# Opening on unscaled rows: the norm's factor applied behind the transposes and behind the first two projections

## The reference

```python
def rmsnorm(x, g):
    y = x * rsqrt(mean(x * x, axis=-1) + EPS)
    return y * g

h = rmsnorm(x, norm1_g)
z = h @ w_in                      # 1024 x 2824
u_s5, x_rg, g_rg, q, k, v, o, gi, gf = split(z)
mix = concat(s5(u_s5), rglru(x_rg, g_rg), mlstm(q, k, v, gi, gf, o))
x = x + mix @ w_out
x = x + moe(rmsnorm(x, norm2_g))  # top 4 of 32 experts
y = rmsnorm(x, final_norm_g)
# S5's coefficients, from small weights only:
step = exp(log_step)
mag = exp(lam_re * step)
ab = mag * cos(lam_im * step), mag * sin(lam_im * step)
```

## Time and profile before

| | us |
|---|---|
| runs, median of 3 | 1101.66 (1099.63 to 1101.93) |
| profiled execution | 1100.9 |
| its span | 1099.1 |

### The profile page before, as it was taken

How to read it: one execution, slowest core, us unless ns; L and a number is a source line. 1 busy time by engine, 2 the same in 40 slices (tenths; PEclk the granted TensorE clock), 3 DMA queues, 4 the chain that set the end, 5 groups by cost and what they waited for, 6 DMA issues and landing times.

```text
span 1099.1 us, 13174 instructions
## 1 busy us (share of the span) xinstructions
PE 1033.2 (94%) x5132; PEld 434.6 (40%) x5132; DVE 317.2 (29%) x643; ACT 198.4 (18%) x418; POOL 95.4 (9%) x177
## 2 busy tenths in 40 slices
PE   8999999999999998999899988999899989998986
PEld 5767745334333433343333323332334233433322
DVE  6889456312131212120212112121212121202123
ACT  6543525301110201011000201020102010100002
POOL 6899000000000000000000000000000000000000
PEclk9999999999999999999999999999999999999999
DMA  7533799999999999999999999999999999999995
GB/s 234 185 111 78 271 370 401 426 428 431 431 431 430 429 432 432 432 431 431 432 431 432 431 431 432 432 431 431 432 432 432 431 431 432 432 431 431 425 427 202
DMA packets 62052, 429.45 MB, mean 391 GB/s; under 512 B 12022, under 2 KB 25054, under 8 KB 33342
## 3 DMA queue, kind: packets, MB, share of 16 engines
q1 hardware_dynamic: 60868, 428.16, 93.3%
q10 hardware_dynamic: 1146, 0.79, 0.2%
HBM read 424.68 MB, written 3.67 MB: 390 GB/s over the span
## 4 chain that ended last, share of the span: by engine, by line
PE 53%; DMA 38%; DVE 5%; ACT 2%; issue 1%; SPq 1%; ACTq 0%; DVEq 0%
DMA ring_a<-in_exp_w_dram 32%; PE psum L2369 17%; PE psum L2404 12%; PE psum L2390 6%; DMA ring_b<-in_exp_w_dram 6%; PE psum L2303 3%; PE psum L2326 3%; PE psum L2134 3%; PE psum L1862 2%; PE psum L2413 1%; PE psum L2253 1%; PE psum L2259 1%; DVE rgb L1336 1%; SPq L444 1%; PE psum L2419 0%
## 5 line engine op out<-in xcount | busy, mean ns | idle before, releaser
L2369 PE MATMUL psum<-ring_a,xg 128*64 128x512 f32 x1200 | 341.8, 600 | 14.8 <-DMA ring_a<-in_exp_w_dram 14.8
L2404 PE MATMUL psum<-ring_a,aT 128*64 128x512 f32 x768 | 217.7, 596 | 9.9 <-DMA ring_a<-in_exp_w_dram 9.6
L2369 PEld LDWEIGHTS psum<-ring_a,xg 128*64 128x64 f32 x1200 | 102.8, 137 | 170.8 <-issue 165.4
L2369 PE MATMUL psum<-ring_b,xg 128*64 128x512 f32 x368 | 152.3, 598 | 7.7 <-DMA ring_a<-in_exp_w_dram 7.7
L1667 DVE TENSOR_TENSOR x<-x,psum 128x512 f32<-128x512 f32 x64 | 44.0, 687 | 384.1 <-PE psum L2326 384.1
L2390 PE MATMUL psum<-ring_a,xg 128*64 128x512 f32 x336 | 103.5, 609 | 14.5 <-DMA ring_b<-in_exp_w_dram 14.5
L2404 PEld LDWEIGHTS psum<-ring_a,aT 128*64 128x64 f32 x768 | 68.2, 137 | 111.8 <-issue 106.5
L2404 PE MATMUL psum<-ring_b,aT 128*64 128x512 f32 x256 | 104.1, 595 | 4.0 <-DMA ring_a<-in_exp_w_dram 2.5
L1736 DVE TENSOR_SCALAR acts<-psum 128x512 f32<-128x512 f32 x32 | 22.0, 687 | 224.4 <-PE psum L2390 208.0
L1040 ACT ACTIVATE acts<-acts 128x512 f32<-128x512 f32 x32 | 20.1, 627 | 297.5 <-DVE acts L1736 297.5
L2369 PEld LDWEIGHTS psum<-ring_b,xg 128*64 128x64 f32 x368 | 43.1, 136 | 75.5 <-issue 63.6
(11 more groups left out here) (504 smaller groups left out, 922.8 us busy)
## 6 DMA issues: line engine op xcount, KB each, us to landing
ring_a<-in_exp_w_dram SPq DMA_DIRECT2D x144, 2048.0 KB, 26.3
ring_b<-in_exp_w_dram SPq DMA_DIRECT2D x46, 2048.0 KB, 24.9
ring_a<-in_w_in_dram SPq DMA_DIRECT2D x4, 2048.0 KB, 8.5
ring_a<-in_w_out_dram SPq DMA_DIRECT2D x2, 2048.0 KB, 9.1
ring_a<-in_w_in_dram SPq DMA_DIRECT2D x3, 1024.0 KB, 5.8
ring_a<-in_state_ml_c_dram SPq DMA_DIRECT2D x4, 512.0 KB, 6.1
out_dram<-ring_a SPq DMA_DIRECT2D x4, 512.0 KB, 6.2
ring_b<-in_exp_w_dram SPq DMA_DIRECT2D x2, 1024.0 KB, 28.9
```

What stands on the lines that cost most here:

```text
L2369: m = M(psum[64 * x:64 * x + 64, bk, :], xg[:, k, u, 64 * x:64 * x + 64], w[x][:, 512 * bk:512 * bk + 512], start=False, stop=(k == KD - 1))
L2404: m = M(psum[64 * x:64 * x + 64, 4 + nn, :], aT[:, 2 * j + s, 64 * x:64 * x + 64], w[x][:, 1024 * s + 512 * nn:1024 * s + 512 * nn + 512], ...
```

## The change

TensorE turns the rows as they land, unscaled. All six halves are moved by VectorE, times the norm's weight, into `raw_hT`, which lies in the room of the later `qkT`. The root is taken once for all three tiles and inverted once. TensorE multiplies the factors, spread over 128 columns, by the identity: the bank rstd then holds in each partition the factor of each of the 288 rows. ScalarE copies it to `rstd_row`. VectorE multiplies `raw_hT` by it in two halves into `hT` (`scaled`). u0 and u1 are projected from `raw_hT` and scaled by VectorE as it moves them (`u_scaled`); ScalarE makes the rolled copy from `uT`. All later projections read `hT`.

The vectors are turned in two tiles: 24 rows and the S5 step first (`vec`), the others inside u0 (`vec2`). The step's exponential is taken on the two partitions of `step2` before it is spread. The matmuls of `keep_warm` go from 14, 1, 1 and 2 to 9 and 1. The left half of the first weights is issued ahead of five of the vector loads, the two lambdas ahead of both, the states' loads go from SyncE's queue to ScalarE's, the S5 output weights (`glw`) behind one block of input weights, and par is turned after xr0. The row's multiplications stand on VectorE between the angles and the coefficients for the first half, u0 and the second half; u1 stands behind the coefficients.

```diff
@@ -68,7 +69,9 @@
 _fills_of[b] += 1
-_place(["vec"] + [f"hT{i}" for i in range(6)] + ["u0", "u1", "par", "gp", "xr0", "gates", "xr1", "bt", "gr0", "ct", "gr1"], range(6))
+_place(["vec", "vec2"], (6,))
+_place(["rstd"], (7,))
+_place([f"hT{i}" for i in range(6)] + ["u0", "u1", "par", "gp", "xr0", "gates", "xr1", "bt", "gr0", "ct", "gr1"], range(6))
@@ -181,6 +183,7 @@
 hT = ms("hT", [128, KD, T])
+raw_hT = qkT[:].rearrange("p (k t) -> p k t", k=KD)
@@ -211,6 +214,7 @@
 uT_rolled = ms("uT_rolled", [128, 2, T])
+rstd_row = uT_rolled[:, 1, :]
@@ -458,6 +462,9 @@
     sp.dma_start(xn[0:TS, 2, :], a["x_sample"].rearrange("b t n -> (b t) n")).then_inc(sem("x_loaded2"), 16)
+    for name, src in LAMBDAS:
+        load_vector(sp, name, src)
+    sp.dma_start(slot_view(0, 512)[:, :, 0:256], w_in_cols(WCH[0][0], 256)).then_inc(sem("w_in0"), 16)
@@ -471,15 +478,10 @@
                     sp.dma_start(c_in[:, 2 * x + tt, :], a[name][0, 8 * tt:8 * tt + 8].rearrange("g c p -> (g c) p")).then_inc(sem("c_loaded"), 16)
-            for x, name in enumerate(("state_s5_re", "state_s5_im")):
-                sp.dma_start(srow[64 * x:64 * x + 64, :], a[name][0].rearrange("b (j g) p -> (b j) (g p)", g=2)).then_inc(sem("par_loaded"), 16)
-            sp.dma_start(prow[0:32, :], a["state_ml_n"][0].rearrange("b h k -> (b h) k")).then_inc(sem("par_loaded"), 16)
...
             sp.dma_start(m0[:], a["state_ml_m"][0].rearrange("b h -> h b")).then_inc(sem("gb_loaded"), 16)
+        if c == 2:
             sp.dma_start(glw[:], a["s5_glu_w"][0].rearrange("(k p) n -> p k n", p=128)).then_inc(sem("glw_loaded"), 16)
-        if c == 2:
@@ -494,9 +496,7 @@
         if c == 0:
-            for x in range(2):
-                sp.dma_start(slot_view(0, 512)[:, :, 256 * x:256 * x + 256], w_in_cols(WCH[0][0] + 256 * x, 256)).then_inc(
-                    sem(("w_in0", "w_in0_right")[x]), 16)
+            sp.dma_start(slot_view(0, 512)[:, :, 256:512], w_in_cols(WCH[0][0] + 256, 256)).then_inc(sem("w_in0_right"), 16)
@@ -655,6 +655,7 @@
     pool.wait_ge(*fill_ended("hT5"))
+    pool.wait_ge(*at("root_ready", 1))
@@ -722,32 +723,33 @@
     act.wait_ge(*at("nst_set", 1))
-    A(nst[:, 12:13], nst[:, 8:9], ACT.Sqrt).then_inc(says_now("table_loaded"), 1)
+    act.wait_ge(sem("step_loaded"), 16)
+    A(step2[:], step2[:], ACT.Exp).then_inc(sem("step_exp"), 1)
...
         A(x1[0:n, i, :], xn[0:n, i, :], ACT.Square, accum_out=nst[0:n, i:i + 1]).then_inc(says_now("ms_ready"), 1)
-        act.wait_ge(*at("ms_ready", i + 1))
-        A(nst[:, 4 + i:5 + i], nst[:, i:i + 1], ACT.Sqrt, scale=1.0 / D, bias=nst[:, 8:9]).then_inc(says_now("root_ready"), 1)
-    await_fill(act, "vec")
-    A(vecs[:, 0:NVEC + J5], bank("vec")[:, 0:NVEC + J5], ACT.Copy).then_inc(drained[FILLS["vec"][0]], 1)
-    act.wait_ge(drained[FILLS["vec"][0]], 1)
-    for i in range(2):
-        name = f"hT{2 * i + 1}"
-        await_fill(act, name)
-        for c in range(4):
-            m = A(hT[:, 4 + c, 128 * i:128 * i + 128], bank(name)[:, 128 * c:128 * c + 128], ACT.Copy, scale=vec("norm1_g", 4 + c))
-        m.then_inc(drained[FILLS[name][0]], 1)
+    act.wait_ge(*at("ms_ready", 3))
+    A(nst[:, 4:7], nst[:, 0:3], ACT.Sqrt, scale=1.0 / D, bias=nst[:, 8:9]).then_inc(says_now("root_ready"), 1)
     act.dma_start(bias_in[:, 0:512], a["exp_b1"][0].rearrange("e (q n) -> q e n", q=4)).then_inc(sem("bias_loaded"), 16)
-    act.dma_start(bias_in[:, 512:768], a["exp_b2"][0].rearrange("e (q n) -> q e n", q=4)).then_inc(sem("bias_loaded"), 16)
-
-    A(sm[:, 1, :], vecs[:, NVEC:NVEC + J5], ACT.Exp).then_inc(says_now("step_ready"), 1)
-    act.wait_ge(*at("angle_reduced", 1))
+    await_fill(act, "vec2")
+    A(vecs[:, NFIRST:NVEC], bank("vec2")[:, NFIRST:NVEC], ACT.Copy).then_inc(drained[FILLS["vec2"][0]], 1)
+    act.wait_ge(drained[FILLS["vec2"][0]], 2)
+
+    act.wait_ge(sem("mag_arg"), 1)
...
     A(g_exp[:, 12:14], rsm[:, 0:2], ACT.Exp, scale=-1.0).then_inc(says_now("act_rg"), 1)
+    copy_out("rstd", rstd_row, bank("rstd")[:, 0:T])
+    act.wait_ge(*at("angle_reduced", 1))
...
     A(sm[:, 7, :], sm[:, 8, :], ACT.Sin).then_inc(says_now("angle_ready"), 1)
+    act.dma_start(bias_in[:, 512:768], a["exp_b2"][0].rearrange("e (q n) -> q e n", q=4)).then_inc(sem("bias_loaded"), 16)
+    for x, name in enumerate(("state_s5_re", "state_s5_im")):
...
+    act.dma_start(prow[0:32, :], a["state_ml_n"][0].rearrange("b h k -> (b h) k")).then_inc(sem("par_loaded"), 16)
@@ -758,17 +760,14 @@
     def u_out(x):
-        await_fill(act, f"u{x}")
+        act.wait_ge(sem("u_scaled"), x + 1)
         for half_ in range(2):
-            A(uT_rolled[64 * half_:64 * half_ + 64, x, :], bank(f"u{x}")[64 - 64 * half_:128 - 64 * half_, 0:T], ACT.Copy).then_inc(
+            A(uT_rolled[64 * half_:64 * half_ + 64, x, :], uT[64 - 64 * half_:128 - 64 * half_, x, :], ACT.Copy).then_inc(
                 sem("u_rolled"), 1)
-        act.wait_ge(sem("u_rolled"), 2 * x + 2)
-        copy_out(f"u{x}", uT[:, x, :], bank(f"u{x}")[:, 0:T])
     u_out(0)
+    u_out(1)
     bias_piece(0)
-    u_out(1)
-    copy_out("par", parT[:, 0:224], bank("par")[:, 0:224])
@@ -777,6 +776,7 @@
     xp_out(0)
+    copy_out("par", parT[:, 0:224], bank("par")[:, 0:224])
@@ -1228,23 +1228,20 @@
     V.tensor_reduce(part_sums, ident[:].rearrange("p (j c) -> p c j", j=4)[:, 0:2 * H], AX.X, ALU.add).then_inc(sem("part_sums_ready"), 1)
-    for i, (t0, n) in enumerate(TILES):
-        dve.wait_ge(*at("root_ready", i + 1))
-        dv(V.reciprocal(nst[:, 4 + i:5 + i], nst[:, 4 + i:5 + i]))
-        says(TSC(xn[0:n, i, :], xn[0:n, i, :], nst[0:n, 4 + i:5 + i], None, ALU.mult), "xn_ready", i + 1)
     says(V.memset(v2[:, 128:129], 1.0), "ones_ready", 1)
-    dve.wait_ge(drained[FILLS["vec"][0]], 1)
-    for k in (0, 2, 4, 5):
+    await_fill(dve, "vec")
+    dv(V.tensor_copy(vecs[:, 0:NFIRST], bank("vec")[:, 0:NFIRST]))
+    drains(V.tensor_copy(sm[:, 1, :], bank("vec")[:, NFIRST:NFIRST + J5]), "vec")
+    for k in (0, 1, 2, 4, 3, 5):
...
         await_fill(dve, f"hT{k}")
-        drains(TT(hT[:, 4 * hf:4 * hf + 4, t0:t0 + n], bank(f"hT{k}").rearrange("p (k n) -> p k n", k=4)[:, :, 0:n],
+        drains(TT(raw_hT[:, 4 * hf:4 * hf + 4, t0:t0 + n], bank(f"hT{k}").rearrange("p (k n) -> p k n", k=4)[:, :, 0:n],
...
     lr, li = vec("s5_lambda_re"), vec("s5_lambda_im")
-    dve.wait_ge(*at("step_ready", 1))
-    dv(TT(sm[:, 2, :], lr, sm[:, 1, :], ALU.mult))
+    TT(sm[:, 2, :], lr, sm[:, 1, :], ALU.mult).then_inc(sem("mag_arg"), 1)
...
+    V.reciprocal(nst[:, 4:7], nst[:, 4:7]).then_inc(sem("rstd_ready"), 1)
+
+    def scaled(hf):
+
+        k = slice(4 * hf, 4 * hf + 4)
+        TT(hT[:, k, :], raw_hT[:, k, :], spread(rstd_row.unsqueeze(1), 1, 4), ALU.mult).then_inc(sem("hT_scaled"), 1)
+
+    def u_scaled(x):
+
+        await_fill(dve, f"u{x}")
+        TT(uT[:, x, :], bank(f"u{x}")[:, 0:T], rstd_row, ALU.mult).then_inc(sem("u_scaled"), 1)
+        dve.wait_ge(sem("u_scaled"), x + 1)
+        dve.sem_inc(drained[FILLS[f"u{x}"][0]], 1)
+
+    dve.wait_ge(drained[FILLS["rstd"][0]], 1)
+    scaled(0)
+    u_scaled(0)
+    scaled(1)
@@ -1277,6 +1293,8 @@
     dv(TT(sm[:, 13, :], sm[:, 13, :], sm[:, 14, :], ALU.mult))
+    u_scaled(1)
+    dve.wait_ge(drained[FILLS["vec2"][0]], 2)
@@ -1813,41 +1831,53 @@
     pe.wait_ge(sem("warm_ready"), 1)
-    keep_warm(14)
+    keep_warm(9)
...
         t0, n = TILES[i]
-        pe.wait_ge(*at("xn_ready", i + 1))
-        await_bank(pe, f"hT{k}")
+        pe.wait_ge(sem(f"x_loaded{i}"), 16)
...
     turn_half(1)
-    keep_warm(1)
-    pe.wait_ge(sem("vec_loaded"), 16 * 11)
-    TR(bank("vec")[:, 0:NVEC], vrow[0:NVEC, :], ident[0:NVEC, 0:NVEC])
+    pe.wait_ge(sem("vec_first"), 16 * 3)
+    TR(bank("vec")[:, 0:NFIRST], vrow[0:NFIRST, :], ident[0:NFIRST, 0:NFIRST])
     pe.wait_ge(*at("ind2_ready", 1))
-    pe.wait_ge(sem("step_loaded"), 16)
-    ends_fill(M(bank("vec")[:, NVEC:NVEC + J5], ind2[:].rearrange("g x p -> g (x p)"), step2[:], start=True, stop=True), "vec")
+    pe.wait_ge(sem("step_exp"), 1)
+    ends_fill(M(bank("vec")[:, NFIRST:NFIRST + J5], ind2[:].rearrange("g x p -> g (x p)"), step2[:], start=True, stop=True), "vec")
...
         turn_half(k)
+
+    def rows_turned(hf):
+
+        for i in range(len(TILES)):
+            b, f = FILLS[f"hT{2 * i + hf}"]
+            pe.wait_ge(drained[b], f + 1)
+
+    def scale_spread(k):
+
         if k == 3:
-            keep_warm(1)
-    keep_warm(2)
-    for k in range(6):
-        b, f = FILLS[f"hT{k}"]
-        pe.wait_ge(drained[b], f + 1)
-
-    def channels(name, c, col, between=None):
+            rows_turned(1)
+        if k == 4:
+            pe.wait_ge(sem("vec_loaded"), 16 * 8)
+            await_bank(pe, "vec2")
+            ends_fill(TR(bank("vec2")[:, 0:NVEC], vrow[0:NVEC, :], ident[0:NVEC, 0:NVEC]), "vec2")
+        if k == 5:
+            pe.wait_ge(sem("rstd_ready"), 1)
+            for i, (t0, n) in enumerate(TILES):
```

(22 more changed lines are left out.)

20 lines of the change are left out of this document (11 added, 9 removed).

## The result

The changed kernel takes 1109.88 us (median of 4 runs, 1108.88 to 1112.95) against 1100.78 us before (4 runs, 1099.63 to 1101.93): a ratio of 1.0089 with a 95% interval of 1.0076 to 1.0101. It is 9.1 us slower, where I had forecast 2.4, and 1109.9 lies outside my range. (The forecast of 1104.1 us starts from 1101.66, the median of three runs; with the fourth it is 1100.78.) The profiled execution took 1109.82 us with a span of 1108.0 us (before: 1100.9 and 1099.1).

A forecast was written before the change was run, and what follows sets the result against it. Expert weights' stream sets the pace; its start hangs on VectorE's chain from L1264. Terms 1.66 + 0.54 + 0.2 = 2.4 us later, on the median of 1101.66, gave 1104.1 us, range 1101.2 to 1106.8.

The forecast's parts named there:

- Steps 1 to 7: Opening up to VectorE's coefficients: first projection 2.2 us sooner, VectorE's chain from L1264 1.66 us later, second scaled eviction 0.54 more.
- A: Opening: Exp table loaded early, so the scale hides under the Sin table; 1102.6 us, chance 0.15.
- steps 5 and 6: Spread row copied from 15.6 us after Exp's table load (1.28 us); Sins end at 17.65, L1264 starts 1.66 us later.
- Step 8: Port contention between GpSimd's table chain and VectorE's second large multiplication: +0.2 us, between nothing and 1.4.
- D: VectorE catches up by meeting shorter GpSimd operations: about 2 us come back, 1101.8 us, chance 0.10.
- The sentence behind the sum: TensorE's start, 2.2 us sooner, only lengthens its wait at 75 us, from 1.4 to about 4.5 us.
- B: First projection at TensorE's lower clock, 1.2 instead of 2.4 GHz: +4.9 us, 1106.6 us, chance 0.10.
- One for one: Every microsecond lost on VectorE from L1264 on reaches the end in full; TensorE's gains ahead of 95 us are worth nothing.
- step 9: Items costed at nothing: state loads on ScalarE's queue, gate products' wait, roll of u, reordered loads; covered by TensorE's lead.

The follow-up runs named there:

- a_fill_hold: Changed kernel with twelve extra TensorE products ahead of the first scan's products and GpSimd's table held until both multiplications are done: 1104.72 us, ratio 1.0045.
- a_hold: Changed kernel with GpSimd's table of rotations held until VectorE has done both multiplications by the spread row: 1105.14 us, ratio 1.0044.
- b_shift2: Kernel before with a 2.0 us filling instruction on VectorE ahead of L1264 and GpSimd's table held until it is done: 1106.03 us, ratio 1.0046.
- a_fill: Changed kernel with twelve extra TensorE products, whose result nobody reads, in the wait ahead of the first scan's products: 1106.75 us, ratio 1.0062.
- b_pool2: Kernel before with GpSimd's table alone held until VectorE's eighth small instruction from L1264 on: 1102.09 us, ratio 1.0011.
- b_fill: Kernel before with the twelve extra TensorE products alone, ahead of the first scan's products: 1105.75 us, ratio 1.0043.
- b_shift2_fill6: Kernel before with VectorE and GpSimd both 2.0 us late and six extra TensorE products ahead of the first scan's products: 1103.41 us, ratio 1.0030.
- a_noscale: Changed kernel with its two multiplications by the spread row cut from 1152 elements a partition to 8: 1109.93 us, ratio 1.0073.

## Why the prediction was wrong

**Steps 1 to 7 held.** First projection 10.74 us (10.7 forecast), copy of the spread row 15.58 (15.6), magnitude chain 19.14 (19.4), +1.35 (+1.66), the second scaled eviction 0.76 with its wait (0.54), together 2.11 us (2.20). No rival on the opening came true: the Exp table was loaded behind the vectors, not ahead (A). ScalarE's first activation started 1.3 us behind the start of each table load (13.84 to 15.13, 15.98 to 17.28 us), as steps 5 and 6 took it.

**Step 8 was mis-sized.** I took +0.2 us for the port and bounded it at 1.4, from the overlap of GpSimd's first short operations with one multiplication. That overlap did happen and fell on GpSimd, by its timeline in the changed kernel (L664; the same copy, L663 before, took 0.20 us):

```profile
17.98 1.30 POOL L664 COPY tabc<-sm 128x8 f32<-128x8 f32 x1
```

But the table chain runs beside VectorE until about 70 us, and a delay of VectorE alone shifts every meeting of the two. Here VectorE, then GpSimd, both of the changed kernel:

```profile
44.89 0.98 DVE L1379 COPY cvfin<-ring_a 128x24 f32<-128x24 f32 x1
...
46.11 0.90 DVE L1379 COPY cvfin<-ring_a 128x24 f32<-128x24 f32 x1
```

```profile
44.80 1.04 POOL L679 TENSOR_TENSOR ring_a<-tabc,sm 128x512 f32<-128x512 f32 x1
45.92 1.06 POOL L680 TENSOR_TENSOR ring_a<-tabc,sm 128x512 f32<-128x512 f32 x1
```

The two copies took 0.18 us each in the kernel before, by VectorE's timeline:

```profile
43.18 0.18 DVE L1361 COPY cvfin<-ring_a 128x24 f32<-128x24 f32 x1
```

The term measured 1.55 + 1.20 = 2.75 us. For the 1.55 a_fill_hold and a_hold show that it is GpSimd's place and not lateness; for the 1.20 they point the same way (nothing in a_fill_hold, 0.51 in a_hold), but other kernels with GpSimd held lose up to 1.1 us there, so that part is less sure. I had this thought, with the opposite sign, as D; the row of 0.90 us was its price, and nothing in the profile told the sign. (D's own sum was off too: six operations at 0.90 less 0.42 us are 2.9 us, not 2.)

**The sentence behind the sum failed.** "On TensorE the start sooner by 2.2 us turns into a longer wait" was costed at nothing. Forecast 4.5 us, the wait was 6.83, and it brought the lower clock (1.94 us) and the locked rounds (2.38). Nor was it the sooner start that made it long: 0.57 us of that was left, and 4.88 were VectorE's lateness. With step 8 sized rightly the term would still have been missing, for in b_shift2 the clock fell behind a wait of 3.02 us. B had the mechanism, but I placed it at the first projection, where a wait of 1.31 us stood before, and not where I myself forecast the longest wait. a_fill, which fills that wait, adds 6.4 us instead of 9.1, and is 5.23 instead of 9.20 us late at TensorE's first product by the mask. That the low clock causes the lock rests on the order in the trace (TensorE late, VectorE waits, GpSimd waits for VectorE, both released by one scan) and on six profiles against fourteen; no run let the clock fall and broke the lock.

**"One for one" failed on both sides.** A delay of 1.0 us cost 7.8 and one of 2.0 cost 9.8, with nothing of the change; starts 0.6 and 1.7 us earlier gave nothing. My reading that VectorE alone orders the time from 17.79 us on overlooked that its results from TensorE (the gates' product at 27.6 us, L1942's at 44.0) come just in time, which a chain without waits doesn't show.

**B in its own place** is real too, but not in the changed kernel's own profile: of nine profiles of it and its variants four had a granted clock near 0.50 in the first projection. There it delays the vectors that are turned inside that projection, and VectorE's chain with them (3.85 to 5.65 us late instead of 2.1 to 2.8 where the multiplications stand). It also uncovers a term of step 9: in all four TensorE waits 0.86 to 2.25 us, up to 29.3 to 30.5 us, for the last of the state loads that went to ScalarE's queue (L1990 above), and then the granted clock falls once more, to 0.50 or 0.52 in a window of two us between 32 and 36 us. In the changed kernel's own profile that load lands some 24.8 us after the start, half a microsecond ahead of its use at 25.31 us: costed at nothing it was right there, but with hardly any cover. In four of eleven profiles of the kernel before and its variants the clock fell at about the same time, but the chain's start didn't move (-0.05 us in b_pool2, 0.06 in b_fill), since nothing on it waits for that projection. What decides between fall and no fall in the opening stays open; so does whether the slowest of the changed kernel's four runs (1112.95 us) is such a case.

The Trainium skill ("SBUF — State Buffer", SBUF: two separate sides) calls the port an exclusive lock that whoever starts first holds. The rows agree: GpSimd's copy of 1.30 us beside the multiplication, and VectorE's 1.79 us whenever GpSimd's product starts 0.03 or 0.04 us ahead of it.

Open remains what the change costs with all of this covered (between 0.3 and 5.2 us), and why b_shift2_fill6 lost 0.8 us between its first product of B and its first S5 value: its VectorE is busy 20.11 us behind the first scan of the gates, against 19.17 in the kernel before, although GpSimd was held.

## What to carry to other kernels

Before a delay is costed one for one, look at three things that it moves: how the delayed engine falls against the engine that shares its port, how long the engine that waits for it will be idle and at what clock it will then run, and whether two engines will from then on be released by the same event. A chain without waits on one side and waits of about 1 us on the other is a balance, and both directions must be tried; a hold of GpSimd by some 2 us took away a growth of 2.8 us on VectorE (a_fill and a_fill_hold), more than the 2.11 us of work that was added. Size a filler by its records in the trace, not by its instructions.

## What the runs showed of the hardware

- Ahead of the first scan, the granted clock fell in or behind TensorE waits of 2.19, 2.75, 3.02, 4.81, 6.61 and 6.83 us, to 0.50 to 0.54 in the lowest window of two us, and was back at 1.00 some 3 to 7 us later; with waits of 0.79 to 1.63 us it stayed at 1.00. The length of one wait doesn't decide alone: in the opening of the kernel before and its variants the clock fell behind waits of 1.28 to 1.31 us in four of eleven profiles but stayed at 1.00 behind 1.31 us in the kernel before itself, and in a_noscale at 30 us behind one of 0.86 us.
- A VectorE instruction of 128x384 took 0.56 to 0.85 us freely and 1.77 to 1.80 when GpSimd's product of 128x576 started just ahead of it (0.03 or 0.04 us in the changed kernel), and the rounds of the two engines, 5.1 to 5.3 us each in the kernel before, took 6.19 to 6.21 us when locked.
- In f32 a product of 288 columns is two records on TensorE, 0.25 us each at a granted clock of 1.00: twelve products took 5.98 us, six 3.07.
